# Value and filler products as two 64-column halves, one accumulator bank a unit, in a fused attention, Fourier and feed-forward layer on eight cores

## The chip, the cores and the metric

The kernel runs on the 8 cores of one Trainium2 chip, one batch element on each core, with no exchange between cores. The metric is the time of one execution on the device in microseconds (us), that of the slowest core. Engines are named as in the profile: PE is TensorE (PEld its weight loads), ACT is ScalarE, DVE is VectorE, POOL is GpSimd, SP is SyncE, which here only issues DMAs.

## The reference, cut to what matters

For each batch element, `x` is 2048 x 1024 and the context is 256 x 1024. Both are RMS-normalised and modulated by vectors computed from a condition.

```python
qx, kx, vx, fx, glx = split_in_proj(h_x @ w_in)      # 16 query heads, 4 key/value heads, width 64
kc, vc = jnp.split(h_c @ w_in[:, Q_W:V_END], 2, -1)  # context: keys and values alone
# q, k: RMS norm per head; rotary for the latent tokens
s = jnp.einsum('bqkgd,btkd->bkgqt', q_blk, k).astype(jnp.float32) * scale
p = jax.nn.softmax(s, axis=-1).astype(v.dtype)       # over 2048 + 256 keys
attn = jnp.einsum('bkgqt,btkd->bqkgd', p, v)
four = Re(fft2(fx)) per channel group                # over positions and channels
merged = g_attn * (attn @ w_attn_proj) + g_four * (four @ w_fourier_proj)
x = x + gt_m * (merged @ w_o)
x = x + gt_f * swiglu(modulate(rms_norm(x)), w_gate_up, w_down)
out = rms_norm(x, g_final)
```

## The kernel before, in words

**A planner writes the order.** The program calls helpers (`mm`, `mms`, `act`, `tt`, `load` and so on); each records a node with its engine, an assumed cost and what it reads and writes. `Tracker.schedule` then simulates the five engines and, whenever one is free, starts the ready node of lowest `prio` (its number in program order plus `late`). The order so found is written out as a fixed instruction stream for each engine; at run time each engine takes its stream strictly in order and waits at each unmet semaphore. A node of PE that carries another `mode` than the one before it is charged `SWITCH_NS` (L69). A load with `after=[v]` also waits for the last writer of `v`; without it, and with no earlier user of its buffer, it is ready at time zero. Since all helpers record one line each, a line in the profile is that of a helper: L396 is `mm` (whole 128x128 weights), L402 is `mms` (several matmuls as one node), L430 transposes, L451 ACT activations, L455 `tt` on DVE, L486 copies and L479 `stt` on DVE, L294 a DMA issue; L286 and L289 are waits.

**Opening.** Sixteen tiles of 128 tokens of `x` and two of the context are loaded on SP's queue into ten buffers `xr` (`xload`), normalised and transposed (`P1`, two tiles a call), modulated by `MOD` (four tiles a call), and projected to keys and values by `KV`. The weights (`w_ada` in four halves, then `w_kv`, `w_q`, `w_f`) come on POOL's queue. `load_tabq(0)` and `load_tabq(1)` load two tables of the queries' rotary and scale them on DVE with `stt` (L479). Four `b_ada` loads of `ada_late_rows` (256 KB each, one row broadcast to all partitions) belong to work inside the attention, but have no `after`.

**Attention.** There are 32 units (four blocks `qb` of 512 queries, eight pairs of heads `c`), each with 18 steps `kt` of 128 keys: `qk(n + 2)` makes the scores of two heads as four 64x64 matmuls (two key halves by two heads) in one of two pairs of banks; ACT takes the exponential of 128 x 1024 scores into one of seven buffers `PTs`; every second step `av(n - 1)` and `av(n)` multiply by the values and `pair_add` (DVE) adds the exponentials up in groups, for the softmax's denominators. `av` is also four 64x64 matmuls: the key rows are split in two, row half `r` accumulates in bank 4 + r. At the end of a unit `finish_unit` copies bank 4 and adds bank 5 on DVE; then come `den` (sums over partitions, as matmuls with 2 columns), `turn` and `scale`. The fillers (projections of later queries and of the Fourier branch, the DFT, the late `ada` products, part of the mixing) are called with `K.level = 2`, which gives their PE nodes the lowest priority; they use banks 6 and 7.

**Tail.** The rest of the mixing, the output projection and the feed-forward network follow, in whole 128x128 matmuls.

Of the kernel before, what the change touches and what calls it, by code (L numbers as in the profile page):

```python
# [62 lines left out]
class Tracker:  # L63
# [2 lines left out]
    LOW = 1 << 20  # L66
    MIX = 1 << 21
    LAST = 1 << 22
    SWITCH_NS = 105.0  # L69
    AHEAD_NS = 130.0  # L70

    def __init__(self):
# [227 lines left out]
def build(debug=False):  # L300
# [60 lines left out]
    def bank(b, nb=1):  # L361
        return View(PS[:, b * 512:(b + nb) * 512], "ps", b * 2048, (b + nb) * 2048)
# [4 lines left out]
    def sub(v, ap):  # L367
        return View(ap, v.sp, v.lo, v.hi)

    def rng(v, ap, elo, ehi, es_):  # L370
        return View(ap, v.sp, v.lo + elo * es_, v.lo + ehi * es_)
# [23 lines left out]
    def mm(out, lhsT, rhs, start, stop):  # L395
        return K.op("pe", lambda h: h.matmul(out.ap, lhsT=lhsT.ap, rhs=rhs.ap, start=start, stop=stop),  # L396
                    reads=[lhsT, rhs], writes=[out], cost=max(30.0, 2.0 + 0.418 * fsz(rhs)))

    def mms(parts, mode=0, cost=None):
        def fn(h):  # L400
            for o_, l_, r_, st_, sp_ in parts:
                ins = h.matmul(o_.ap, lhsT=l_.ap, rhs=r_.ap, start=st_, stop=sp_)  # L402
            return ins
        if cost is None:
            cost = sum(max(30.0, 2.0 + 0.418 * fsz(p[2])) for p in parts)
        reads, seen = [], set()
        for p in parts:
            for v in (p[1], p[2]):
                if (v.sp, v.lo, v.hi) not in seen:
                    seen.add((v.sp, v.lo, v.hi))  # L410
                    reads.append(v)
        writes, seen = [], set()
        for p in parts:
            if (p[0].lo, p[0].hi) not in seen:
                seen.add((p[0].lo, p[0].hi))
                writes.append(p[0])
        return K.op("pe", fn, reads=reads, writes=writes, cost=cost, mode=mode)

    def half(b, h):
        lo = b * 2048  # L420
        return View(PS[h * 64:(h + 1) * 64, b * 512:(b + 1) * 512], "ps", lo, lo + 2048)

    def group(b, nk, lhs, rhs, more=False):
        for k in range(nk):
            mm(bank(b), lhs(k), rhs(k), k == 0, k == nk - 1 and not more)

    def trs(pairs, ident):
        def fn(h):
# [69 lines left out]
    def load(dst, src_ap, q="sp", after=()):  # L498
        return K.dma(q, q, dst.ap, src_ap, after=after, writes=[dst], nbytes=(dst.hi - dst.lo) * 128)
# [129 lines left out]

    def load_tabq(qb):  # L630
        tq = tabqs[qb % 2]
        load(tq, ropeq_d[qb].rearrange("p (a b c) -> p a b c", a=4, b=2))
        t3 = sub(tq, tq.ap.rearrange("p a b c -> p (a b) c"))
        stt("dve", t3, t3, 0.125, sub(gq_bc, gq_bc.ap.unsqueeze(1).to_broadcast([128, 8, 64])), ALU.mult, ALU.mult)

# [17 lines left out]
    def hchunk(tb, k):  # L653
        o = tb * 4096 + k * 512
        return rng(hT, hT.ap[:, tb, k, :], o, o + 512, 2)
# [179 lines left out]
    def dft_pos(fg):  # L835
        ga = lambda a, lt: rng(G, G.ap[:, fg, a, lt, :], (fg * 4 + a) * 512, (fg * 4 + a + 1) * 512, 2)
        tab, alt, altc, GX = DF["tab"], DF["alt"], DF["altc"], DF["GX"]
        gx = rng(GX, GX.ap[:, fg, :], fg * 128, fg * 128 + 128, 2)

        yv = rng(YT, YT.ap[:, fg, :], fg * 2048, (fg + 1) * 2048, 2)  # L840
        y2 = YT.ap[:, fg, :].rearrange("p (n two) -> p n two", two=2)
        yrev = lambda lo, n: bass.AP(YT.ap.tensor, YT.ap[:, fg, lo:lo + 1].offset, [list(YT.ap.ap[0]), [-2, n]])
        for h in range(2):
            qh = dtmp[h]
            b = next_bank()
            group(b, 4, lambda k: ga(2 + h, k), lambda k: tab(2 + h, k))
            cp("act", qh, bank(b))
            b = next_bank()
            group(b, 4, lambda k: ga(h, k), lambda k: tab(h, k), more=h == 0)
            if h == 0:  # L850
                mm(bank(b), gx, alt, False, True)
            pp = bank(b)
            tt("dve", sub(yv, y2[:, 0:512, h]), pp, qh, ALU.subtract)
            if h == 0:
                tt("dve", sub(yv, yrev(2046, 511)), sub(pp, pp.ap[:, 1:512]), sub(qh, qh.ap[:, 1:512]), ALU.add)
            else:
                tt("dve", sub(yv, yrev(2047, 512)), pp, qh, ALU.add)
        px = bank(next_bank())
        mms([(sub(px, px.ap[:, 0:1]), ga(0, lt), sub(altc, altc.ap[:, 0:1]), lt == 0, False) for lt in range(4)]
            + [(sub(px, px.ap[:, 0:1]), gx, sub(alt, alt.ap[:, 0:1]), False, True)])  # L860
        cp("dve", sub(yv, YT.ap[:, fg, 1024:1025]), sub(px, px.ap[:, 0:1]))
# [72 lines left out]

    def ada_late_rows(gt, v, hf):
        g_half = rng(gt, gt.ap[:, hf * 512:(hf + 1) * 512], hf * 512, hf * 512 + 512, 4)
        load(g_half, bada_d[v * 1024 + hf * 512:v * 1024 + hf * 512 + 512].partition_broadcast(128))
        s_ = ada_next()
        pb = bank(next_bank())
        for k in range(8):  # L940
            mm(pb, sub(scond_bc, scond_bc.ap[:, k, :]), sub(s_, s_.ap[:, k, :]), k == 0, k == 7)
        tt("dve", g_half, pb, g_half, ALU.add)
        if v == 2:
            ts("dve", g_half, g_half, 0.5, ALU.mult)
# [77 lines left out]
    def av(n):  # L1022
        qb, c, kt = steps[n]
        pt = PTs[n % NPT]
        p = c // 4
        parts = []
        for r in range(2):
            for h in range(2):
                hd = 2 * p + h
                l_ = rng(V, V.ap[r * 64:(r + 1) * 64, kt, hd * 64:hd * 64 + 64], kt * 256, kt * 256 + 256, 2)  # L1030
                parts.append((half(4 + r, h), l_, sub(pt, pt.ap[r * 64:(r + 1) * 64, h * 512:(h + 1) * 512]),
                              kt == 0, kt == NKT - 1))
        mms(parts, mode=1, cost=216.0)

    sum_i = [0]
    HX = 3
# [2 lines left out]
    def pair_add(n):  # L1039
        qb, c, kt = steps[n]  # L1040
        i = kt // 2
        a, b = PTs[(n - 1) % NPT], PTs[n % NPT]
        if i == 0:
            cur["sums"] = []
        if i % HX == 0:
            slot = sums[sum_i[0] % NSUM]
            sum_i[0] += 1
            cur["sums"].append(slot)
            tt("dve", slot, a, b, ALU.add, per=0.52)
        else:  # L1050
            slot = cur["sums"][-1]
            tt("dve", slot, slot, a, ALU.add, per=0.52)
            tt("dve", slot, slot, b, ALU.add, per=0.52)

    ends = []

# [3 lines left out]

    def finish_unit(qb, c):
        xs = xss[c % 2]
        cp("dve", xs, bank(4), late=PX)
        tt("dve", xs, xs, bank(5), ALU.add, late=PX)
        ss, i = cur["sums"], c % 2
        part = [rng(rh[i], rh[i].ap[:, a, :], a * 8, a * 8 + 8, 2) for a in range(3)]

        def den():
            b = next_bank()
            K.level = 1  # L1070
            for g in range(8):
                mms([(sub(bank(b), bank(b).ap[:, g * 2:g * 2 + 2]), sub(s_, s_.ap[:, g * 128:(g + 1) * 128]),
                      sub(ones, ones.ap[:, 0, 0:2]), k == 0, k == len(ss) - 1) for k, s_ in enumerate(ss)], cost=27.0 * len(ss))
            K.level = 0
            r0, r1 = rr[i], rt[i]
            recip(r0, sub(bank(b), bank(b).ap[:, 0:16].rearrange("p (g n) -> p g n", n=2)[:, :, 0]), late=L_)
            cp("dve", part[0], r0, late=L_)
            tt("dve", r1, r0, part[0], ALU.subtract, late=L_)
            cp("dve", part[1], r1, late=L_)
            tt("dve", part[2], r1, part[1], ALU.subtract, late=L_)  # L1080

        def turn():
            b1 = next_bank()
            K.level = 1
            pt_ = sub(bank(b1), bank_bf(b1).ap[0:24, 0:128])
            trs([(pt_, sub(rh[i], rh[i].ap.rearrange("p a g -> p (a g)")))], ident)
            K.level = 0
            cp("dve", rT[i], pt_, late=L_)

        def scale():  # L1090
            b2 = next_bank()
            K.level = 1
            mms([(sub(bank(b2), bank(b2).ap[:, t * 128:(t + 1) * 128]), sub(sel, sel.ap[:, t, :]), rT[i], True, True) for t in range(4)])
            K.level = 0
            at = attnTs[qb]
            tt("dve", rng(at, at.ap[:, c, :], c * 512, c * 512 + 512, 2), xs, bank(b2), ALU.mult, late=L_)

        ends.extend(zip(DS, (den, turn, scale)))
        credit[0] -= 6
# [13 lines left out]
    PX = -300  # L1113
# [323 lines left out]
```

How the kernel before makes its waits and increments, by code:

```python
    def replay_one(self, nc, name, h, sems, dma_sems):  # L282
        for it in self.plan[name]:
            if it[0] == "wait_op":
                p = it[1]
                h.wait_ge(sems[p.eng], p.num)
            elif it[0] == "wait_dma":
                _, pool, si, val = it
                h.wait_ge(dma_sems[pool][si], val)
            else:
                n = it[1]
                if n.kind == "dma":
                    out_ap, in_ap, pool = n.dma
                    h.dma_start(out=out_ap, in_=in_ap).then_inc(dma_sems[pool][n.tk[1]], 16)
                else:
                    ins = n.fn(h)
                    if n.inc:
                        ins.then_inc(sems[n.eng], 1)
```

## Time and profile before

| | us |
|---|---|
| median of 3 runs | 1549.5 |
| lowest and highest | 1548.71, 1552.95 |
| the profiled execution | 1551.35 |
| its slowest core (core 6), first to last instruction | 1549.8 |
| its other cores | 1536.9 to 1547.7 |

The profile is that of core 6. PE is busy for 1363.4 us (88% of the span), DVE for 840.0 and ACT for 839.3 (54% each). A busy share is an average over stages that have different limits, so the stages are read one by one below: the opening, until the first exponential of the attention; the attention; and the tail. A wait is written behind an instruction as [idle time <- who ended it].

### The profile page before, as it was taken

What the parts mean: (1) busy time and instruction counts of PE and PEld (TensorE: products, weight loads), DVE (VectorE), ACT (ScalarE), POOL (GpSimd) and SP (SyncE); (2) the same over time, 40 slices, a digit from 0 to 9 for tenths busy, and PEclk for the clock granted to TensorE, in tenths of its full rate; (3) what the DMA queues carried; (4) which work ended last, traced back from release to release, by engine and by line L of the source; (5) the groups of instructions that cost most, each with busy time, mean ns of one, the idle gap of its engine ahead of it and who ended that gap; (6) DMA issues with size and microseconds to landing.
All of it is one profiled execution on the core that took longest, in us unless ns stands there. A gap on an engine that the chain in (4) does not pass through costs nothing.

```text
span 1549.8 us, 32186 instructions; the slowest of 8 cores (1536.9 to 1549.8 us)
## 1 busy us (share of the span) xinstructions
PE 1363.4 (88%) x10352; PEld 575.4 (37%) x10352; DVE 840.0 (54%) x1503; ACT 839.3 (54%) x1135; POOL 34.0 (2%) x75
## 2 busy tenths in 40 slices
PE   1267887999788798889999999998999999999997
PEld 1254232333222233223333444443444444444443
DVE  2157788898867788566776433376221112213443
ACT  4285898998877798678998222266311111111111
POOL 0000000000000000000000000000000000000000
PEclk9978899999987999979999999999999999999999
DMA  9840000011112123020122253058145232112222
GB/s 215 237 87 2 8 2 7 3 29 29 29 29 56 29 56 76 2 49 13 38 49 49 49 103 102 1 158 275 44 82 99 39 69 56 28 55 82 109 111 80
DMA packets 20795, 102.05 MB, mean 66 GB/s; under 512 B 3197, under 2 KB 3350, under 8 KB 15510
## 3 DMA queue, kind: packets, MB, share of 16 engines
q0 software_dynamic: 5616, 50.86, 17.8%
q1 hardware_dynamic: 15014, 49.14, 9.0%
q8 instruction: 86, 1.41, 0.4%
q14 instruction: 79, 0.65, 0.1%
HBM read 134.06 MB, written 16.78 MB: 97 GB/s over the span
## 4 chain that ended last, share of the span: by engine, by line
PE 70%; ACT 11%; issue 7%; DVE 6%; SPq 4%; DMA 2%; ACTq 0%; DVEq 0%; POOLq 0%; POOL 0%
PE PS L396 50%; PE PS L402 18%; ACT SB L451 10%; DVE SB L455 4%; SPq L294 4%; DMA SB<-x 2%; PE PS L430 1%; ACT SB L485 1%; DVE SB L495 0%; DVE SB L486 0%; DVE SB L471 0%; ACTq L286 0%; DVE SB L492 0%; DVEq L286 0%; DVE SB L479 0%
## 5 line engine op out<-in xcount | busy, mean ns | idle before, releaser
L396 PE MATMUL PS<-SB 128*128 128x512 bf16 x3752 | 899.5, 384 | 6.0 <-DVE SB L492 2.5
L451 ACT ACTIVATE SB<-PS 128x1024 bf16<-128x1024 f32 (+1 forms) x705 | 625.8, 963 | 319.8 <-PE PS L396 252.9
L396 PEld LDWEIGHTS PS<-SB 128*128 128x128 bf16 x3752 | 358.4, 98 | 537.6 <-issue 164.0
L402 PE MATMUL PS<-SB 64*64 64x512 bf16 (+3 forms) x6132 | 473.6, 356 | 95.4 <-ACT SB L451 51.0
L455 DVE TENSOR_TENSOR SB<-SB 128x1024 bf16<-128x1024 bf16 (+7 forms) x755 | 471.6, 645 | 88.6 <-ACT SB L451 48.2
L455 DVE TENSOR_TENSOR SB<-PS,SB 128x512 f32<-128x512 f32 (+3 forms) x262 | 173.1, 674 | 413.2 <-PE PS L396 343.6
L402 PEld LDWEIGHTS PS<-SB 64*64 64x64 bf16 (+1 forms) x6132 | 184.3, 106 | 319.1 <-issue 296.0
L451 ACT ACTIVATE SB<-SB 128x8 f32<-128x8 f32 (+4 forms) x201 | 106.2, 537 | 232.0 <-DVE SB L455 160.4
L430 PE MATMUL PS<-SB 128*128 128x128 bf16 (+1 forms) x468 | 49.3, 247 | 76.3 <-DVE SB L455 34.4
L451 ACT ACTIVATE SB<-PS,SB 128x512 f32<-128x512 f32 x64 | 44.1, 689 | 122.9 <-PE PS L396 118.4
L479 DVE SCALAR_TENSOR_TENSOR SB<-SB,PS 128x512 f32<-128x512 f32 x64 | 43.9, 686 | 101.6 <-PE PS L396 98.8
L485 ACT COPY SB<-PS 128x1024 bf16<-128x1024 bf16 (+2 forms) x91 | 66.8, 752 | 25.5 <-PE PS L430 19.2
L430 PEld LDWEIGHTS PS<-SB 128*128 128x128 bf16 (+1 forms) x468 | 34.8, 109 | 108.7 <-issue 105.8
L455 DVE TENSOR_TENSOR SB<-SB,PS 128x512 bf16<-128x512 f32 (+1 forms) x64 | 43.5, 680 | 4.5 <-PE PS L402 2.7
L479 DVE SCALAR_TENSOR_TENSOR SB<-SB 128x1024 f32<-128x1024 f32 (+2 forms) x23 | 23.5, 1028 | 37.2 <-DMA SB<-rope_q 34.3
L486 DVE COPY SB<-PS 24x128 bf16<-24x128 bf16 (+1 forms) x72 | 34.0, 472 | 3.7 <-PE PS L430 1.3
L495 DVE TENSOR_REDUCE SB<-SB 128x8 f32<-128x512 f32 x41 | 27.7, 675 | 0.0
L471 DVE TENSOR_SCALAR SB<-SB 128x512 bf16<-128x512 bf16 (+1 forms) x72 | 23.9, 399 | 3.2 <-ACT SB L485 2.3
L469 DVE TENSOR_SCALAR SB<-SB 128x1024 bf16<-128x1024 f32 (+2 forms) x19 | 12.8, 685 | 20.3 <-ACT SB L451 18.2
L492 DVE RECIPROCAL SB<-PS 128x8 f32<-128x8 f32 x32 | 6.5, 203 | 28.5 <-PE PS L402 28.3
L294 POOL DMA_DIRECT2D SB<-w_ada x12 | 6.9, 580 | 473.9 <-PE PS L402 235.2
L294 POOL DMA_DIRECT2D SB<-w_gu x11 | 5.8, 528 | 348.3 <-PE PS L396 227.3
(19 smaller groups left out, 70.9 us busy)
## 6 DMA issues: line engine op xcount, KB each, us to landing
SB<-x SPq DMA_DIRECT2D x32, 512.0 KB, 10.2
SB<-w_mix POOLq DMA_DIRECT2D x8, 1792.0 KB, 12.4
SB<-w_ada POOLq DMA_DIRECT2D x12, 1024.0 KB, 8.0
SB<-w_gu POOLq DMA_DIRECT2D x11, 1024.0 KB, 7.7
x_scratch<-SB SPq DMA_DIRECT2D x16, 512.0 KB, 4.2
SB<-x_scratch SPq DMA_DIRECT2D x16, 512.0 KB, 3.2
out<-SB SPq DMA_DIRECT2D x16, 512.0 KB, 2.6
SB<-w_dn POOLq DMA_DIRECT2D x2, 2048.0 KB, 13.6
```

The costliest lines, as they stand in the source:

```text
L294: h.dma_start(out=out_ap, in_=in_ap).then_inc(dma_sems[pool][n.tk[1]], 16)
L396: return K.op("pe", lambda h: h.matmul(out.ap, lhsT=lhsT.ap, rhs=rhs.ap, start=start, stop=stop), reads=[lhsT, rhs], writes=[out], cost=ma ...
L402: ins = h.matmul(o_.ap, lhsT=l_.ap, rhs=r_.ap, start=st_, stop=sp_)
L430: ins = h.transpose(out=o_.ap, in_=i_.ap, identity=ident.ap)
L451: return K.op("act", lambda h: h.activation(out=out.ap, in_=in_.ap, func=func, **kw), reads=reads, writes=writes, cost=ecost("act", in_), ...
L455: return K.op(eng, lambda h: h.tensor_tensor(out=out.ap, in0=a.ap, in1=b.ap, op=op), reads=[a, b], writes=[out], cost=(1600.0 if op == ALU ...
L469: return K.op(eng, lambda h: h.tensor_scalar(out=out.ap, in0=a.ap, scalar1=a1, scalar2=None, op0=op0), reads=reads, writes=[out], cost=eco ...
L471: return K.op(eng, lambda h: h.tensor_scalar(out=out.ap, in0=a.ap, scalar1=a1, scalar2=a2, op0=op0, op1=op1), reads=reads, writes=[out], c ...
L479: return K.op(eng, lambda h: h.scalar_tensor_tensor(out=out.ap, in0=a.ap, scalar=sa, in1=b.ap, op0=op0, op1=op1), reads=reads, writes=[out ...
L485: return K.op("act", lambda h: h.copy(out=out.ap, in_=in_.ap), reads=[in_], writes=w, cost=ecost("act", in_), late=late)
L486: return K.op(eng, lambda h: h.tensor_copy(out=out.ap, in_=in_.ap), reads=[in_], writes=w, cost=ecost(eng, out), late=late)
L495: return K.op("dve", lambda h: h.tensor_reduce(out=out.ap, in_=in_.ap, axis=AX.X, op=ALU.add), reads=[in_], writes=[out], cost=ecost("dve" ...
```

## The change

- `av` becomes two matmuls, one for each head, over all 128 key rows with 64 weight columns each; both accumulate in the one bank 4 + c % 2, so consecutive units take turns between banks 4 and 5. The two row halves and their two banks are gone.
- The matmuls of `group`, when called as fillers, and the last product of `dft_pos` are each issued as two matmuls of 64 weight columns over all rows (`mm_cols`) into the two partition halves of the bank. Both these and `av` carry the planner's mode 2; `qk` keeps mode 1 and whole matmuls mode 0. The planner's charge for a change of mode goes from 105 to 134 ns.
- `finish_unit` makes one copy of one bank, with the priority of the unit's other end work, and no addition.
- `pair_add` gets `late=-1500`: of the ready DVE nodes the planner takes these first.
- `load_tabq(0)` and `load_tabq(1)` wait for the last modulated chunk of tiles 4 to 7; each of the four late `b_ada` loads waits for the latest writer of `PTs[0]`.

```diff
-    SWITCH_NS = 105.0
+    SWITCH_NS = 134.0
@@
+    def mm_cols(b, l_, r_, start, stop):
+        mms([(half(b, h), sub(l_, l_.ap[:, h * 64:(h + 1) * 64]), r_, start, stop) for h in range(2)], mode=2, cost=216.0)
+
     def group(b, nk, lhs, rhs, more=False):
         for k in range(nk):
-            mm(bank(b), lhs(k), rhs(k), k == 0, k == nk - 1 and not more)
+            if K.level == 2:
+                mm_cols(b, lhs(k), rhs(k), k == 0, k == nk - 1 and not more)
+            else:
+                mm(bank(b), lhs(k), rhs(k), k == 0, k == nk - 1 and not more)
@@ def load_tabq(qb):
-        load(tq, ropeq_d[qb].rearrange("p (a b c) -> p a b c", a=4, b=2))
+        load(tq, ropeq_d[qb].rearrange("p (a b c) -> p a b c", a=4, b=2), after=[hchunk(1, 7)] if qb < 2 else [])
@@ def dft_pos(fg):
-                mm(bank(b), gx, alt, False, True)
+                mms([(half(b, z), sub(gx, gx.ap[:, z * 64:(z + 1) * 64]), alt, False, True) for z in range(2)], mode=2, cost=216.0)
@@ def ada_late_rows(gt, v, hf):
-        load(g_half, bada_d[v * 1024 + hf * 512:v * 1024 + hf * 512 + 512].partition_broadcast(128))
+        load(g_half, bada_d[v * 1024 + hf * 512:v * 1024 + hf * 512 + 512].partition_broadcast(128), after=[PTs[0]])
@@ def av(n):
-        for r in range(2):
-            for h in range(2):
-                hd = 2 * p + h
-                l_ = rng(V, V.ap[r * 64:(r + 1) * 64, kt, hd * 64:hd * 64 + 64], kt * 256, kt * 256 + 256, 2)
-                parts.append((half(4 + r, h), l_, sub(pt, pt.ap[r * 64:(r + 1) * 64, h * 512:(h + 1) * 512]),
-                              kt == 0, kt == NKT - 1))
-        mms(parts, mode=1, cost=216.0)
+        for h in range(2):
+            hd = 2 * p + h
+            l_ = rng(V, V.ap[:, kt, hd * 64:hd * 64 + 64], kt * 256, kt * 256 + 256, 2)
+            parts.append((half(4 + c % 2, h), l_, sub(pt, pt.ap[:, h * 512:(h + 1) * 512]), kt == 0, kt == NKT - 1))
+        mms(parts, mode=2, cost=216.0)
@@ def pair_add(n):
-            tt("dve", slot, a, b, ALU.add, per=0.52)
+            tt("dve", slot, a, b, ALU.add, per=0.52, late=-1500)
         else:
             slot = cur["sums"][-1]
-            tt("dve", slot, slot, a, ALU.add, per=0.52)
-            tt("dve", slot, slot, b, ALU.add, per=0.52)
+            tt("dve", slot, slot, a, ALU.add, per=0.52, late=-1500)
+            tt("dve", slot, slot, b, ALU.add, per=0.52, late=-1500)
@@ def finish_unit(qb, c):
-        cp("dve", xs, bank(4), late=PX)
-        tt("dve", xs, xs, bank(5), ALU.add, late=PX)
+        cp("dve", xs, bank(4 + c % 2), late=L_)
```

## Rows read from the trace of the kernel before

**Rows 1.** The stages: window, length, busy us (and count) of PE, PEld, DVE, ACT, POOL, PEclk, DMA share, GB/s
```profile
152.00:322.00 170.00, 147.24 (x1533) 51.80 (x1533) 142.23 (x256) 153.33 (x199) 0.35 (x1) 0.95 0.02 5
322.00:508.00 186.00, 159.97 (x1708) 55.15 (x1704) 148.01 (x286) 153.18 (x190) 2.81 (x6) 0.89 0.19 36
508.00:696.00 188.00, 159.63 (x1651) 55.05 (x1643) 138.46 (x261) 151.76 (x185) 2.11 (x4) 0.90 0.20 43
696.00:854.00 158.00, 151.65 (x1577) 50.51 (x1573) 111.44 (x212) 143.38 (x160) 1.58 (x3) 0.99 0.18 37
862.00:1549.80 687.80, 667.81 (x3199) 305.07 (x3197) 232.66 (x354) 158.86 (x261) 22.11 (x50) 0.99 0.33 87
```
**Rows 2.** The opening on SP's queue, in order of time
```profile
12.54 3.99 SPq L294 DMA_DIRECT2D SB<-rope_q  x2
16.62 29.89 SPq L294 DMA_DIRECT2D SB<-b_ada  x4
46.67 0.60 SPq L294 DMA_DIRECT2D SB<-dft_altc  x1
47.48 15.50 SPq L294 DMA_DIRECT2D SB<-x  x6
```
**Rows 3.** Landing after issue: x from 8.7 and 10.0, from 62.5; w_kv from 14.1; b_ada
```profile
L294 SPq DMA_DIRECT2D SB<-x x2: 1018/1144/1269, 8.7 to 10.0; - x2
DMA to landing us min/median/max: 41.1/44.2/47.3
...
L294 SPq DMA_DIRECT2D SB<-x x1: 502/502/502, 62.5 to 62.5; - x1
DMA to landing us min/median/max: 16.4/16.4/16.4
...
L294 POOL DMA_DIRECT2D SB<-w_kv x1: 558/558/558, 14.1 to 14.1; - x1
DMA to landing us min/median/max: 43.9/43.9/43.9
...
L294 SPq DMA_DIRECT2D SB<-b_ada x4: 6272/7666/8015, 16.6 to 38.5; - x4
DMA to landing us min/median/max: 29.8/42.6/49.7
```
**Rows 4.** The opening on DVE and PE, in order of time
```profile
27.88 0.17 DVE L455 TENSOR_TENSOR SB<-PS,SB 128x8 f32<-128x8 f32 x1
62.32 1.29 DVE L479 SCALAR_TENSOR_TENSOR SB<-SB 128x512 f32<-128x512 f32 x2 [34.27 <-DMA SB<-rope_q]
...
70.05 9.61 PE L402 MATMUL PS<-SB 128*128 128x256 bf16 x64 [2.15 <-DVE SB L471]
...
117.51 1.89 PE L396 MATMUL PS<-SB 128*128 128x512 bf16 x8 [0.62 <-ACT SB L485]
```
**Rows 5.** The first exponential, on ACT
```profile
152.11 1.03 ACT L451 ACTIVATE SB<-PS 128x1024 bf16<-128x1024 f32 x1
```
**Rows 6.** A step of the attention on PE (320 to 323 us), in order of time
```profile
321.19 0.39 PE L396 MATMUL PS<-SB 128*128 128x512 bf16 x1
321.54 0.63 PE L402 MATMUL PS<-SB 64*64 64x512 bf16 x8
322.10 0.39 PE L396 MATMUL PS<-SB 128*128 128x512 bf16 x1
322.46 0.41 PE L402 MATMUL PS<-SB 64*64 64x512 bf16 x4
```
**Rows 7.** The tail's long run of whole matmuls, in the chain that ended last
```profile
1091.40 449.81 PE PS L396 x2084
```
**Rows 8.** Groups by form: count, busy us, mean ns, idle us before them and what ended it
```profile
L451 ACT ACTIVATE SB<-PS 128x1024 bf16<-128x1024 f32 x576 | 554.0, 1044 | 58.0 <-DVE SB L486 26.3 <-PE PS L402 18.1 <-DVE SB L455 9.0
L455 DVE TENSOR_TENSOR SB<-SB 128x1024 bf16<-128x1024 bf16 x480 | 325.1, 687 | 62.7 <-ACT SB L451 40.1 <-DVE SB L455 15.1
L402 PEld LDWEIGHTS PS<-SB 64*64 64x64 bf16 x4608 | 107.7, 108 | 224.0 <-issue 209.8
L455 DVE TENSOR_TENSOR SB<-SB,PS 128x512 f32<-128x512 f32 x32 | 21.8, 681 | 1.7
```
**Rows 9.** A stall of all engines in the attention (459 to 470 us)
```profile
459.54 1.04 ACT L451 ACTIVATE SB<-PS 128x1024 bf16<-128x1024 f32 x1
...
463.40 1.29 DVE L455 TENSOR_TENSOR SB<-PS,SB 128x512 f32<-128x512 f32 x2 [2.95 <-ACT SB L451]
...
466.82 1.48 DVE L455 TENSOR_TENSOR SB<-SB 128x1024 bf16<-128x1024 bf16 x3
467.60 1.02 ACT L451 ACTIVATE SB<-PS 128x1024 bf16<-128x1024 f32 x1 [1.56 <-DVE SB L455]
```
**Rows 10.** A later table load, issued with its queue free (183 to 184 us)
```profile
L294 SPq DMA_DIRECT2D SB<-rope_q x1: 350/350/350, 183.6 to 183.6; - x1
DMA to landing us min/median/max: 2.4/2.4/2.4
```

## The prediction

> **What bounds the kernel now.** I read the busy time by stage first, because the whole-span shares hide three regimes [rows 1]. From 862 us on PE is busy for 667.8 of 687.8 us at a granted clock of 0.99. The change touches nothing there, so the tail keeps its time. In the attention (152 to 854 us, 702 us) no engine is full: adding the four stages, ACT is busy for 602 us, PE for 619 and DVE for 540, and the granted clock falls to 0.89 and 0.90 in the middle stages, that is, some stretches run at 1.2 instead of 2.4 GHz. I therefore asked next what an exponential waits for, in the groups by form [rows 8]. The third question was what fills the 152 us before the first exponential [rows 5], where the order of SP's queue shows it.
>
> *The opening.* SP issues two rope_q and four b_ada loads ahead of the last six x loads [rows 2]. The issue of b_ada alone keeps SP for 29.9 us, since the queue is full. The x load issued at 10.0 lands at 10.0 + 47.3 = 57.3 us, and the last b_ada at 38.5 + 29.8 = 68.3. So 11 us of the queue lie between two x loads. The last x load lands at 62.5 + 16.4 = 78.9 [rows 3]. A second cost is on DVE: its next instruction after 28.05 us scales the rope_q table, and waits 34.27 us for it; the normalisation of x tiles 6 and 7, the modulation and with them the first key/value matmuls (70.05 us) are behind it in the order [rows 4]. Their weights w_kv had landed at 14.1 + 43.9 = 58.0 us [rows 3].
>
> *The attention.* The 576 exponentials had 58.0 us of idle ACT before them, of which 26.3 + 9.0 = 35.3 us were ended by DVE [rows 8]. Rows 9 show the form this takes. [rows 9] After the exponential at 459.54 none starts for 8.1 us. DVE stands in its fixed order at a rotary step of a later query tile, waits 2.95 us for ACT, then works through that chain; only at 466.82 does it do the pair sums that free the exponential's output buffer, and the exponential starts at 467.60. PE, which feeds ACT, idles with it.
>
> **The change part by part.**
>
> *Loads.* Four b_ada and two rope_q loads leave the early queue. x, context and everything that follows them there move up by the 11 us that lay between 57.3 and 68.3, and DVE's 34.27 us wait is no longer ahead of the modulation. Then w_kv is the last to come, at 58.0 instead of a start at 70.05: 12 us. Both the last x (11) and the first key/value product (12) move by about the same, so the whole chain up to 152.11 should. I take -12. Bounds: -8, if the chain from 80 us on is already filled by ACT's own work; -18, because ACT also gets copies and scalings of tiles 6 to 9 done while it would wait for x (about 6 us, six such operations of some 1 us). The moved loads must be paid somewhere. The tables are needed from the first query projection, at 117.5 us now [rows 4]; one issued with its queue free landed in 2.4 us [rows 10]. On SP the waiting rope_q issue has at worst the context loads queued behind it, and on DVE its scaling stands ahead of key work: 0, at most +3. The four b_ada loads go into the attention on SP, where little is queued; DVE may wait for each at its addition, with the pair sums behind it: +1 in all, bounds 0 and 4 x 2.4 = +10.
>
> *Pair sums first.* When a sum and another DVE operation are both ready in the plan, the sum goes first. This removes stalls of the form of rows 9. It does not remove those in which DVE already waits at a PE product that comes later than planned, with the sums behind it, because the order stays fixed. I take two thirds of 35.3: -23, bounds -35 and -10. What is late next is the chain of the query rotary, which has slack, and PE.
>
> *One bank a unit.* 32 additions of 0.681 us are gone [rows 8]: 21.8 us of DVE. DVE is busy for only 540 of 702 us, so this is nothing on the path; bounds 0 and -5. The next unit's first `av` no longer waits for the copy and addition of the last, but almost none of it waits today.
>
> *Halves.* No row shows a 64-column matmul over 128 rows. The nearest are the quads of 64x64: eight of them in 322.10 - 321.54 = 0.56 us including the change to a whole matmul [rows 6]; a whole matmul takes 449.81/2084 = 0.216 us [rows 7], and two quads 0.43. So four tiles on two column halves and two row halves run together in the time of one. A pair of halves streams the same rows into the same columns, and I price it at 0.216 us as the whole matmul: 0. If the two ran one after the other, each pair would cost 0.216 more. Weight loads of 64 columns take 108 ns [rows 8] and lie beside the matmuls.
>
> The Trainium skill, "TensorEngine Tiling (Array Packing)", Gotcha 2 of its restrictions, speaks against the halves: column tiling excludes Fast Weight Load, so two half loads could replace a fast whole one. Taken one behind the other at the 108 ns of the trace they would fill 0.216 us, exactly a pair's matmul time, so the rule adds nothing that the rest would need.
>
> *Changes of mode.* A filler between quads costs 0.56 - 0.43 = 0.13 us going in and (322.46 - 322.10) - 0.216 = 0.14 coming out [rows 6], 0.135 a change. Today `qk` and `av` share a mode. I counted the changes in the PE order that the kernel's planner writes for the attention: 988. In the same order with the new modes there are 1311, for a quad of `qk` is now followed by a change even where only `av` comes, while a step with `qk`, `av` and a filler keeps its two. The 323 extra are 44 us of PE. In 69 of the 576 gaps between scores there is nothing but `av`; those have slack (0.43 + 0.27 against ACT's 0.92 a step) and hold 138 of the 323. That leaves 185 x 0.135 = 25 us; PE is the one waited for in about half of the attention, so +12; bounds 0 and +44.
>
> That moving between 64x64 tiles and 128x64 tiles is a change of mode at all is not in any row. The same page of the Trainium skill, under Key Properties, has any change of tiling mode drain TensorE; the trace agrees for 64x64 against 128x128 with its 0.13 and 0.14 us.
>
> *Clock.* In the attention the granted clock was below 1 for (0.05 x 170 + 0.11 x 186 + 0.10 x 188 + 0.01 x 158) x 2 = 99 us at half level [rows 1], at up to half of that lost. Stretches of low PE activity, as in rows 9, come before part of it. Fewer stalls: -6, bounds -20 and +10.
>
> *Sum* against the profiled execution: 1551.35 - 12 + 1 - 23 + 12 - 6 = 1523.4. The median of the runs is 1.85 below that execution, so 1521.5, told as 1521.
>
> **The rivals.**
>
> *A. The opening alone.* The switches and the fixed order eat what the sums give. For it: PE is busy for 151.7 of 158 us in the last quarter. Attention unchanged: 1549.5 - 12 = 1537.5, from 1532 to 1544.
>
> *B. Slower: PE becomes the bound through mode changes.* In a step with one filler PE now needs 0.43 + 0.216 + 0.27 = 0.916 us against ACT's 0.92 [rows 6]; any more makes PE the bound in every such step. If going to and from 128x64 costs 0.05 us more than 0.135 in 1311 places, that is 66 us, plus the 44 of the extra ones, while the removed DVE stalls lie beside it: 1549.5 - 12 + 44 + 66 - 35 = 1612. The point from which it decides is about 50 us of PE time on the path. Against it: each kind of change in the trace costs about the same. With the halves one behind the other (576 pairs of `av` and 657 of fillers at 0.216 us) it would be 266 us more, about 1790.
>
> *C. Free changes.* If the column split and not the row split makes a mode, `qk`, `av` and fillers are one: 324 changes instead of 988, 90 us less PE work, and ACT's 602 us bound the attention. It would take about 640, and the kernel 1549.5 - 12 - 62 = 1475.
>
> *D. The change does not do what it says*: the b_ada or table loads stay early by another way, or hold SP's queue for the x loads. Then the opening stays and 1533 is left.
>
> **How the numbers follow.** Forecast (1488 to 1533) 0.58; A 0.20; D 0.05; B 0.10; C 0.07. The likeliest is 1521. The range leaves out B and C and holds the rest, up to the case in which only the lower bound of the opening is left: 1488 to 1545. About 0.3% (4.6 us) can be told from no change. Faster holds the forecast, C, D and nearly all of A: 0.85. Same takes the rest of A and a mild B: 0.06. Slower 0.09.
>
> **What would show it.** The first exponential at 140 (+-4) us, with no DVE wait for rope_q of more than a few us and the last x landed before 70. In the groups, the exponentials' idle time ended by DVE at 12 us instead of 35.3. The pairs of halves starting a few ns apart, the next pair 0.216 us later. The step of one filler at 0.92 us still. A tail of 688 us. I am wrong if the pair takes more than 0.216, or if the attention is not between 665 and 695 us.

## The result, and the profile after

The changed kernel is slower: 1.0391 times the time of before, 95% interval 1.0347 to 1.0435, that is about 1610 us against 1549.5. Forecast were 1521 us and a range up to 1545. All ratios here leave out executions in which one die ran at a visibly lower clock than the other (the plain median of the changed kernel, 1661.86 us, holds two such). The profiled execution has a span of 1606.2 us on core 2.

The first fence has the stages of the changed kernel (columns as in rows 1), the second the attention as one window, for before and after: first to last exponential.

```profile
144.00:330.00 186.00, 159.24 (x1436) 57.90 (x1434) 139.49 (x252) 157.65 (x203) 0.53 (x1) 0.95 0.03 6
330.00:530.00 200.00, 167.82 (x1516) 61.49 (x1512) 138.61 (x272) 148.91 (x183) 2.64 (x5) 0.85 0.16 31
530.00:750.00 220.00, 184.32 (x1572) 66.75 (x1568) 137.16 (x258) 164.91 (x196) 2.11 (x4) 0.89 0.20 43
750.00:908.00 158.00, 151.28 (x1410) 56.20 (x1408) 103.94 (x201) 134.22 (x150) 1.58 (x3) 0.99 0.20 37
917.00:1606.20 689.20, 666.96 (x3198) 304.99 (x3194) 233.16 (x354) 158.53 (x261) 22.14 (x50) 0.99 0.34 87
```

```profile
152.10:854.90 702.80, 619.39 (x6459) 212.76 (x6459) 540.82 (x1014) 602.45 (x731) 6.85 (x13) 0.93 0.15 30
```

```profile
144.70:909.70 765.00, 663.88 (x5932) 242.97 (x5932) 520.08 (x984) 606.92 (x731) 6.87 (x13) 0.92 0.15 29
```

Of [rows 1] the tail answers as forecast: 689 us against 688. The attention grew from 702.8 to 765.0 us. ACT has the same work (602 and 607 us) and DVE 21 us less, as forecast; PE is busy for 44 us more. The longer time is idle time on ACT (100 us before, 158 now), and the granted clock is as low as 0.85 in one stage.

Two rows of the changed kernel, the exponentials' from the groups by form and the reciprocals' from the page (busy us, mean ns of one, idle us before and who ended it), then the reciprocals' of before:

```profile
L457 ACT ACTIVATE SB<-PS 128x1024 bf16<-128x1024 f32 x576 | 553.8, 1044 | 78.3 <-DVE SB L492 37.0 <-PE PS L402 21.5 <-DVE SB L461 15.5
```

```profile
L498 DVE RECIPROCAL SB<-PS 128x8 f32<-128x8 f32 x32 | 6.5, 204 | 50.5 <-PE PS L402 50.5
```

```profile
L492 DVE RECIPROCAL SB<-PS 128x8 f32<-128x8 f32 x32 | 6.5, 203 | 28.5 <-PE PS L402 28.3
```

The exponentials' idle time ended by DVE did not fall from 35.3 us [rows 8] to 12, it rose to 52.5. The reciprocal is the first DVE step after `den`. DVE's idle time before it, nearly all of it ended by PE, went from 28.5 to 50.5 us. That row leads to the cause. It was in the page of before, and the prediction did not use it.

**Opening.** SP now has the last six x loads right behind the others, and the first key/value product waits for w_kv alone. In order: the loads, PE's first key/value product and DVE, all on core 2, then the first exponential on core 6, the core of [rows 5].

```profile
13.33 34.13 SPq L294 DMA_DIRECT2D SB<-x  x6
```

```profile
59.03 9.68 PE L402 MATMUL PS<-SB 128*128 128x256 bf16 x64 [5.81 <-DMA SB<-w_kv]
```

```profile
55.37 0.74 DVE L475 TENSOR_SCALAR SB<-SB 128x1024 bf16<-128x1024 f32 x1
75.13 1.29 DVE L461 TENSOR_TENSOR SB<-PS,SB 128x512 f32<-128x512 f32 x2 [19.02 <-ACT SB L457]
```

```profile
141.48 1.03 ACT L457 ACTIVATE SB<-PS 128x1024 bf16<-128x1024 f32 x1
```

The product starts at 59.03 instead of 70.05 [rows 4], 11 us earlier as forecast. Then DVE waits 19.02 us for ACT, which takes the squares of the x tiles still arriving before that of the first keys. The last x tile landed at 70.0 us instead of 78.9. Over the eight cores the median start of the first exponential moved from 147.9 to 142.1 us: 6 us, not 12.

**A stall like that of [rows 9], in the changed kernel**, in order of time:

```profile
564.00 1.92 PE L402 MATMUL PS<-SB 128*64 128x512 bf16 x16
...
566.02 0.60 ACT L457 ACTIVATE SB<-PS 128x512 f32<-128x512 f32 x1 [3.38 <-PE PS L402]
566.72 1.29 DVE L461 TENSOR_TENSOR SB<-PS,SB 128x512 f32<-128x512 f32 x2 [1.25 <-ACT SB L457]
...
568.16 0.74 PE L402 MATMUL PS<-SB 128*128 128x2 bf16 x24 [2.24 <-DVE SB L461]
...
568.75 0.60 ACT L457 ACTIVATE SB<-SB 128x8 f32<-128x8 f32 x2 [2.13 <-DVE SB L501]
569.46 1.29 DVE L461 TENSOR_TENSOR SB<-SB 128x512 bf16<-128x512 f32 x2 [0.25 <-ACT SB L457]
...
570.67 0.20 DVE L498 RECIPROCAL SB<-PS 128x8 f32<-128x8 f32 x1
570.84 1.02 ACT L457 ACTIVATE SB<-PS 128x1024 bf16<-128x1024 f32 x1 [1.49 <-DVE SB L461]
570.85 0.69 DVE L461 TENSOR_TENSOR SB<-SB 128x1024 bf16<-128x1024 bf16 x1
```

A bank is one of the eight 512-column parts of `PS`, into which PE writes. Read backwards. The exponential at 570.84 needs its output buffer, which a pair sum must have read. That sum is the second of the two DVE operations from 569.46 on: the view merges them under the shape of the first, and they end at 570.75. The sum writes one of six slots, two units' worth, and must wait until `den` (24 matmuls with 2 columns, 568.16 to 568.90) has read that slot for the unit before last. `den` writes one of banks 6 and 7. The planner keeps the accesses to a bank in program order, so `den` waits until the filler called before it has been computed (564.00) and read out of its bank by DVE (566.72, two operations in 1.29 us). The fillers have the lowest priority and lag; as soon as they lag too far, the unit end lags with them, and two units later the exponentials stop. Call this theory W.

No exponential runs from 562.65 to 570.84. Of these 8.2 us only 1.49 are counted in front of the exponential; 3.38 and 2.13 stand in front of the two operations of a filler that ACT had ahead of it in its order. So the sum in front of the exponentials understates such stalls: of ACT's 58 us more of idle time it has 20.

In [rows 9] the two operations at 463.40 (1.29 us together) are such a read-out, not steps that happen to stand ahead of the sums. `den` follows them at once:

```profile
464.84 0.74 PE L402 MATMUL PS<-SB 128*128 128x2 bf16 x24 [2.30 <-DVE SB L455]
```

### The profile page after: what moved, and what is told of

Its sections match the earlier page's. It is cut to its first block, busy times and chain, and to the rows that moved or that the text cites. A ratio compares the mean times of both kernels' runs of the same rounds, so it can differ in the third digit from the quotient of the medians.

```text
span 1606.2 us, 31068 instructions; the slowest of 8 cores (1598.7 to 1606.2 us)
## 1 busy us (share of the span) xinstructions
PE 1408.4 (88%) x9844; PEld 606.4 (38%) x9844; DVE 818.7 (51%) x1471; ACT 843.8 (53%) x1135; POOL 34.0 (2%) x75
## 4 chain that ended last, share of the span: by engine, by line
PE 69%; ACT 12%; issue 7%; DVE 6%; DMA 4%; SPq 0%; ACTq 0%; DVEq 0%; POOLq 0%; POOL 0%
PE PS L396 39%; PE PS L402 29%; ACT SB L457 11%; DVE SB L461 4%; DMA SB<-x 4%; PE PS L436 1%; ACT SB L491 1%; DVE SB L501 1%; DVE SB L477 0%; SPq L294 0%; DVE SB L492 0%; ACTq L286 0%; DVEq L286 0%; DVE SB L485 0%; ACT L457 0%
## 5 line engine op out<-in xcount | busy, mean ns | idle before, releaser
L402 PE MATMUL PS<-SB 64*64 64x512 bf16 (+5 forms) x6268 | 690.5, 365 | 120.1 <-ACT SB L457 41.2
L396 PE MATMUL PS<-SB 128*128 128x512 bf16 x3108 | 682.8, 380 | 1.0 <-ACT SB L491 0.6
L461 DVE TENSOR_TENSOR SB<-SB 128x1024 bf16<-128x1024 bf16 (+7 forms) x755 | 464.7, 645 | 80.1 <-ACT SB L457 43.6
L402 PEld LDWEIGHTS PS<-SB 64*64 64x64 bf16 (+2 forms) x6268 | 269.9, 107 | 530.1 <-issue 489.7
L396 PEld LDWEIGHTS PS<-SB 128*128 128x128 bf16 x3108 | 302.8, 98 | 367.6 <-issue 12.1
L491 ACT COPY SB<-PS 128x512 bf16<-128x512 bf16 (+2 forms) x91 | 67.1, 752 | 28.1 <-PE PS L436 14.3
L498 DVE RECIPROCAL SB<-PS 128x8 f32<-128x8 f32 x32 | 6.5, 204 | 50.5 <-PE PS L402 50.5
L461 DVE TENSOR_TENSOR SB<-SB,PS 128x512 bf16<-128x512 f32 x32 | 21.8, 682 | 14.6 <-PE PS L402 14.6
```

Source lines behind the costliest of these rows:

```text
L461: return K.op(eng, lambda h: h.tensor_tensor(out=out.ap, in0=a.ap, in1=b.ap, op=op), reads=[a, b], writes=[out], cost=(1600.0 if op == ALU ...
L491: return K.op("act", lambda h: h.copy(out=out.ap, in_=in_.ap), reads=[in_], writes=w, cost=ecost("act", in_), late=late)
```

## The experiments

All kernels were timed against the kernel before. Two theories were put first: **M**, each change of tiling on PE costs 0.125 us on the path; **S**, the priority of the sums does the harm. Then **W**, and last **O** (the loss sits in the order that the planner writes).

**1. The edits one by one.** The loads alone, the kernel before with:

```diff
+ after=[hchunk(1, 7)] if qb < 2 else []   # load_tabq
+ after=[PTs[0]]                           # b_ada
```

> The kernel before with the two load edits alone (the rotary tables wait for the modulated chunk, b_ada for PTs[0]). Both theories: only the opening moves. In the changed kernel the first exponential came at 144.7 instead of 152.1 us, so 7.4 us earlier; here the same, 1549.5 - 7.4 = 1542 us, ratio 0.995. If the late b_ada loads hold DVE in the attention, part of it is given back and the ratio is above 0.997.

Measured 0.9951 (0.9932 to 0.9970): 7.6 us less.

```diff
+ late=-1500     # the three tt of pair_add
```

> The kernel before with late=-1500 on the pair sums alone. Theory M (changes of PE mode make the 60 us): this order has 851 changes in the attention instead of 985, at 0.125 us each 17 us less, and no stall is added: 1530 to 1545. Theory S (the sums' priority starves the rest of DVE's work, on which fillers and the unit ends wait): attention longer by 15 to 40 us, 1565 to 1590, with more idle DVE and PE.

Measured 1.0188 (1.0155 to 1.0220): 29 us more, though the order has fewer changes of tiling. M fails as the only cause. DVE's idle time before the reciprocal is 40.4 us, up from 28.5, so S names the right edit, and W offers the way: sums first means that the operations which empty banks 6 and 7 come later. (The idle time right before the exponentials is about the same, 54.9 us after 58.0. What grew is that before ACT's filler operations.)

```diff
- parts for r in 2, h in 2: half(4 + r, h), 64 rows each; mode=1
+ parts for h in 2: half(4 + c % 2, h), 128 rows; mode=2
- cp(xs, bank(4)); tt(xs, xs, bank(5))
+ cp(xs, bank(4 + c % 2), late=L_)
```

> The kernel before with the value products alone as column halves (one bank a unit, one copy); fillers stay whole, so that qk, av and fillers are three modes. The order has 1587 changes in the attention instead of 985. Theory M: 602 x 0.125 = 75 us of PE work, most of it on the path: 1600 to 1625. Theory S: the changes are hidden, as PE has idle time: 1540 to 1560.

Measured 1.0339 (1.0307 to 1.0370): 53 us more, inside M's range. The signs of W hardly moved here: 33.7 us before the reciprocal, and 36.8 us ended by DVE before the exponentials, after 35.3. PE is busy for 680 us of the attention instead of 619. So this run by itself does not show W.

```diff
+ group at K.level 2 and the last product of dft_pos by mm_cols, mode=2
```

> The kernel before with the fillers alone as column halves; av stays four 64x64 tiles. 1036 changes instead of 985: Theory M: +6 us, 1555, if a pair of halves costs the 0.216 us of a whole matmul. The changed kernel's trace has pairs that follow each other after 0.240 instead of 0.216 us: if that is the price of the halves, 655 x 0.024 = 16 us more, up to 1571. Theory S: no difference but that.

Measured 1.0054 (1.0028 to 1.0079): 8 us more, where M with halves at 0.216 us had 6. In the changed kernel filler pairs follow one another after 0.216 us (564.00 above: eight pairs in 1.92 us, of which 0.40 is the last one's own length), so the halves as such are free. The four runs add up to +82 us; the whole change, which also has the charge of 134 ns, costs 60.6. The costs do not add. One reason is plain: `av` alone makes 1587 changes of mode, while `av` and fillers together make 1338, as they share a mode. A common wait may be another.

**2. The unit end in a bank of its own.** With one bank a unit, bank 4 + c % 2 is idle once it is copied.

```diff
-            b = next_bank()      # den; likewise b1 in turn, b2 in scale
+            b = 4 + c % 2
```

> The changed kernel, with the unit-end matmuls (den, turn, scale) in the unit's own bank 4 + c % 2, which is free once it is copied, instead of the banks 6 and 7 shared with the fillers. Theory W (the exponentials stop because a pair sum waits for its slot until den has read it, and den waits in program order for a filler's bank): the exponentials' idle time ended by DVE falls from 52.5 to under 20 us, the attention from 765 to 700 to 720 us; about 145 filler products then come after the last exponential, some 31 us more there: 1570 to 1590. Theory M alone (mode changes fill PE): no change beyond 5 us.

Measured 1.0029 (1.0018 to 1.0039): 1554 us, 56 less than the changed kernel from this edit alone, more than expected. The attention took 677.5 us, and what followed the last exponential 730 instead of 696 us: by the two orders 145 filler products more come after it. First the exponentials and the reciprocals, then the attention as one window.

```profile
L457 ACT ACTIVATE SB<-PS 128x1024 bf16<-128x1024 f32 x576 | 544.1, 1052 | 9.2 <-PE PS L402 7.8
L498 DVE RECIPROCAL SB<-PS 128x8 f32<-128x8 f32 x32 | 6.4, 201 | 1.4 <-PE PS L402 1.4
```

```profile
143.80:821.30 677.50, 606.94 (x5673) 229.49 (x5673) 519.36 (x975) 589.97 (x721) 5.51 (x11) 0.96 0.13 25
```

No exponential waits for DVE any more to speak of, and of the 60.6 us some 56 are gone. That the bank shared with the fillers carries this loss is shown. The edit also makes the planner write another order, so the wait at run time and the order that plans for it are not told apart.

**3. The priority again.** The changed kernel without it:

> The changed kernel without the priority of the pair sums. Alone the priority cost 1.9% over the kernel before. If that is because it delays the DVE work that frees the fillers' banks (W), it costs here too: 15 to 25 us less, 1580 to 1590. If it only used up idle time that the mode changes now fill: within 5 us of the changed kernel.

Measured 1.0270 (1.0243 to 1.0296): 19 us less than with it. The kernel before with `late=-60` instead:

> The kernel before with the pair sums 60 places earlier instead of 1500, which puts them ahead of the DVE work of the same steps but not of that of fillers called several steps before. W: no loss, 1545 to 1556. If being first in itself does the harm (DVE stands at a sum whose exponential is late): half of the 29 us or more, 1565 and above.

Measured 0.9987 (0.9975 to 0.9998), as W had it. Being ahead of the same steps' work is harmless; it is the 1500 places, which also pass the read-outs of fillers, that cost 29 us. And with the own bank, without the priority:

> The changed kernel with the unit-end matmuls in the unit's own bank and without the priority of the pair sums. W: the priority did harm only through the wait of den for a filler's bank; with that wait gone, the priority costs nothing: within 5 us of the same kernel with the priority, 1550 to 1559. If the priority harms by itself, as over the kernel before or in the changed one: 12 to 29 us less, 1525 to 1542.

Measured 1.0034 (1.0017 to 1.0052), the same as with it (1.0029). In the changed kernel the priority harms only by way of `den`'s bank.

**4. den at the attention's priority**, in the kernel before with the loads:

```diff
-            K.level = 1          # in den
+            K.level = 0
```

> The kernel before with the two load edits and with den at the attention's own PE priority. W: den's matmuls come earlier in the order, so a slot is free sooner: 3 to 8 us less than the load edits alone (0.9951), ratio 0.990 to 0.993. M: the number of changes falls from 985 to 955, 4 us at 0.125: ratio 0.992. Both faster; it is a candidate for a version that beats both kernels.

Measured 0.9902 (0.9881 to 0.9924): a little faster than both kernels, and 8 us less than the loads alone. Its idle time before the reciprocal is 15.9 us. The ratio fits W and M alike.

**5. Whole fillers beside `av` halves**, with the own bank:

> The same as the run beside it (own bank, no priority, the planner's 134 ns) but with whole fillers, so that qk, av and fillers are three modes: 1460 changes of mode in the order instead of 1373. M: 87 x 0.125 = 11 us more. If the halves of the fillers cost something themselves (0.240 instead of 0.216 us a pair), that is saved: 508 x 0.024 = 12 us less, and the two come out equal.

Measured 1.0199 (1.0170 to 1.0227), 26 us more than its neighbour. Both expectations missed: 1460 instead of 1373 changes do not make 26 us at 0.125. Fewer filler products got into the attention (484 in the order against 508), and it was 14 us longer, the rest after it 11 us. Why stays open.

**6. What a change of tiling costs on the path.** The score product as one pair in the place of four 64x64 tiles, at an unchanged order. The kernel leaves out half of the scores, as the expectation says. In the changed kernel:

```diff
-        for kc in range(2):
-            for h in range(2):
-                ... 64x64 tile (h, kc) into bank b0 + h
+        for kc in range(2):
+            ... 128 rows, 64 columns, into bank b0 + kc
```

> The changed kernel, in exactly its order, with the score product as two matmuls of 64 columns over all 128 rows instead of four 64x64 tiles. It leaves out half of the scores (one head's lower and the other's upper half of the keys are not computed; the rest of each bank is stale) and keeps the time of the product at 0.216 us, while qk, av and the fillers are now one tiling: 350 changes instead of 1338. Theory M: the 988 removed changes at about 0.12 us are 119 us of PE, of which the attention, in steps where PE is waited for, gives back most: 60 to 100 us, 1505 to 1545. Theory W alone (the wait of den, not the changes): less than 15 us.

Two executions took 1586.1 and 1587.5 us, 20 to 25 less than the changed kernel's 1607.8 and 1610.6; there is no interval for this. Both expectations missed: M had 60 to 100 us, W less than 15.

```profile
151.60:889.50 737.90, 588.56 (x4782) 235.66 (x4782) 518.40 (x984) 600.81 (x731) 6.86 (x13) 0.94 0.15 30
```

PE is busy for 75 us less than in the changed kernel, but the attention is only 27 us shorter. The same edit with the own bank:

> The same edit on the kernel whose unit-end matmuls use the unit's own bank (1554 us): half of the scores left out, 458 changes instead of 1354, same order. The exponentials wait for no bank here. If the changes cost only through the fillers' lag and the wait of den, 896 removed ones give less than 20 us. If PE's own time sets the pace of the steps, 40 to 70 us: 1485 to 1515.

Measured 1.0009 (0.9995 to 1.0023), 3 us less than with the changes (1.0029). So M is wrong as a price: the real changes cost 20 us where the unit end shares the fillers' banks and about 3 where it doesn't. What is left for the rest of the halves' cost is the order, in which the fillers are fixed at their late places even if PE now has time. That is argued from what remains; part 7 looks at the order.

**7. The order.** The changed kernel with the planner's charge at 105:

> The changed kernel with the planner's charge for a change of mode back at 105 ns. Two runs have shown that removing 900 to 1000 real changes at an unchanged order gives only 20 and 4 us. Theory O (the order that the planner writes carries the loss: with more changes charged it puts the fillers later and the unit end behind them): a lower charge makes an order with less lag, 5 to 20 us less, 1585 to 1600. If the charge only has to be true to the chip (0.12 us), 105 is no better than 134: within 5 us of 1605, or slower.

Measured 1.0313 (1.0283 to 1.0343), 12 us less than with 134. O holds in this part: nothing on the chip was changed but the order.

The planner has a figure of its own for this, which the forecast did not read: the end time `est_ns` that `Tracker.schedule` computes together with the order. It is 1458 us for the kernel before and 1527 for the changed one, 69 more, where 61 were measured. For the priority of the sums alone it has 40 more (29 measured), for `av` alone 44 (53), for the fillers alone 8 (8). If `av` alone is given the mode of `qk`, so that no change between them is charged, it is 1457: in the plan the charged changes cost, and the products themselves nothing. The figure knows no clock and is no forecast of each kernel (the one of part 2 has +37 in it and +4.5 in the measurement), but the sign and most of the loss stand in the planned order before anything runs.

The kernel of part 4, with the charge at 134 and

```diff
-    AHEAD_NS = 130.0
+    AHEAD_NS = 0.0
```

> The fastest version so far (loads, den at the attention's priority; 0.9902) with the planner's charge at 134 ns and AHEAD_NS at 0: the planner no longer lets PE stand up to 130 ns for a score product that is about to be ready, but takes a filler. 927 changes of mode instead of 955. W and M both: less idle PE, fillers lag less, so den comes earlier: 5 to 15 us less, ratio 0.980 to 0.987. If a filler taken at that moment holds up the next scores by its 0.216 us and two changes, it is slower: above 0.992.

Measured 0.9750 (0.9726 to 0.9774), better than expected; DVE's idle time before the reciprocal is 4.7 us. The kernel of part 3 without the priority and with the own bank, AHEAD_NS 0:

> The kernel of the first run of this set with AHEAD_NS at 0: 1400 changes of mode instead of 1373. More fillers lie in the attention (552 against 508 products), so the rest after it is 44 x 0.216 = 9.5 us shorter, and the attention should not grow by as much: 1535 to 1550, against 1554 with the own bank. If the mode changes set the attention: + 27 x 0.125 + 44 x 0.216 = 13 us there, and no gain in all.

Measured 0.9801 (0.9774 to 0.9828), 1519 us, below the expectation of 1535 to 1550. And with fillers called at `RATE = 1.5` instead of 1.7 as well:

> Own bank, no priority of the sums, AHEAD_NS 0 (ratio 0.9801) with fillers called at 1.5 instead of 1.7 a step, which lowers the changes in the attention from 1400 to 1280 at the same 552 filler products in it. M: 120 x 0.12 = 14 us less, ratio 0.971, which would beat 0.975. If the number of calls does not matter: 0.980.

Measured 0.9631 (0.9603 to 0.9659), 1494 us: 56 us faster than the kernel before. The step from 0.9801 is 26 us, twice what M gave for it. Last, this kernel with the unit end back on banks 6 and 7:

> The fastest kernel (0.9631: own bank for the unit end, no priority of the sums, AHEAD_NS 0, 1.5 filler units a step) with the unit end back on the fillers' banks 6 and 7. W: the exponentials again wait for slots behind den: idle time ended by DVE back above 20 us and 40 to 55 us more, 1530 to 1550. If the other two edits made the gain, it stays within 10 us of 1494.

Measured 1.0223 (1.0197 to 1.0249), 1586 us, beyond the expectation for W. The choice of bank, the same line in three places, is worth 91 us here; the plan's `est_ns` has 54 of them (1442 and 1496). First the fast kernel, then this one, each with its exponentials and reciprocals (groups by form) and the attention as one window.

```profile
L457 ACT ACTIVATE SB<-PS 128x1024 bf16<-128x1024 f32 x576 | 557.6, 1045 | 18.5 <-PE PS L402 9.8 <-DVE SB L461 3.4 <-ACT SB L457 0.8
L498 DVE RECIPROCAL SB<-PS 128x8 f32<-128x8 f32 x32 | 6.4, 201 | 2.4 <-PE PS L402 2.4
```

```profile
146.60:771.70 625.10, 582.09 (x5761) 215.15 (x5761) 515.29 (x980) 597.32 (x724) 5.80 (x11) 0.99 0.15 30
```

```profile
L457 ACT ACTIVATE SB<-PS 128x1024 bf16<-128x1024 f32 x576 | 561.9, 1035 | 63.2 <-PE PS L402 29.4 <-DVE SB L492 18.8 <-DVE SB L461 6.6
L498 DVE RECIPROCAL SB<-PS 128x8 f32<-128x8 f32 x32 | 6.5, 204 | 28.1 <-PE PS L402 27.9
```

```profile
151.90:862.50 710.60, 632.51 (x5724) 227.23 (x5724) 518.11 (x971) 608.29 (x723) 5.80 (x11) 0.90 0.12 26
```

ACT is busy for 597 of 625 us in the fast one: the attention is now bound by it. The granted clock is 0.99 against 0.90, and PE is busy for 50 us less with the same products. The 58 fewer changes of mode are 7 us of that (an estimate at 0.12 us each); most of the rest goes with the clock.

## Why the prediction was wrong, point by point

- **Pair sums first: -23 forecast, +29 alone and +19 in the changed kernel.** This step failed in sign. The forecast took the 35.3 us ended by DVE [rows 8] for sums queued behind other DVE work. The trace names who released a wait, not what that one had waited for. In [rows 9] `den`, which reads the slot that the sum overwrites, ran from 464.84 to 465.58, and the sum began at 466.82. Of the 8.1 us a place further ahead could have saved 1.2 at most. The question left out was "what did the releaser itself wait for", and the reciprocal's 28.5 us answers it.
- **Changes of mode: +12 forecast (0 to +44), of which the halves alone cost 53 (`av`) and 8 (fillers).** The count was near: 1311 forecast, 1338 in the order. The price of one was right too: in the changed kernel a 64x64 quad to a 128x64 pair takes 0.34 us from start to start, 0.216 of it the quad. What failed is that PE's work was set against PE's idle time step by step, at an order taken as given. The order did not stay: the planner, told of 350 more changes, wrote one whose own end time is later. And the fillers may lag by two units at most before the exponentials stop, so what PE loses can come back as a stall. In the changed kernel all 988 real changes around `qk` cost 20 us (part 6), so the 350 extra ones less, and the planner's higher charge 12 (part 7). How the 53 of `av` alone divide was not measured: the signs of W hardly moved in that run, and the plan puts its 44 us down to the charged changes (part 7).
- **Opening: -12 forecast (-18 to -8), 7.6 measured alone.** The mechanism held: the key/value product came 11 us earlier. The lower bound of 8 named the case that came true, ACT's own work, and its size was a little off. Where the 7.6 us lie is less clear: with the loads alone the median start of the first exponential moved by 2 us only (147.9 to 145.9), and the rest was not located.
- **Late loads: +1 and 0, near.** The first table's scaling waits 4.43 us for rope_q, over the bound of 3; how much of it reached the first exponential was not measured. No DVE wait for b_ada shows.
- **Halves at full rate: right.** Pairs follow at 0.216 us. The rule of the Trainium skill on Fast Weight Load ("TensorEngine Tiling (Array Packing)", Gotcha 2) can't be told from these rows, since the loads lie beside the matmuls; the rule that a change of tiling mode drains the engine (same page, Key Properties) agrees with the 0.12 us for 64x64 against 128x64, which no row of before had shown.
- **One bank a unit: 0 forecast, right as the change uses it.** Its worth is that it frees a bank for the unit end, which the change does not use.
- **Clock: -6 forecast.** At half level in the attention: 99 us before, 130 in the changed kernel, 55 with the own bank, 14 in the fastest. The time at half level rose instead of falling. In these four the clock goes with the stalls, but not in all: sums first alone had 96 us at half level and was 29 us slower. What the clock adds by itself was not separated.
- **Rival B** had the sign and the place (extra changes). That its 1612 us is near the 1610 measured is luck: it needs 0.05 us more for each change, which is not there, and 110 us of PE time on the path, where the real changes cost 20.

## What to carry to other kernels

When an engine ends a wait, follow that engine's own wait one step further back, down to the buffer or bank, before pricing a change of priority. Work of low priority must not share a bank, slot or queue with work that the critical loop will need later, as the shared order turns its lag into a stall. A program whose order is fixed by a planner has to be judged by the order it gets: a small change of an assumed cost moved 12 us, and removing about 1000 real changes at an unchanged order 20 or 3. Such a planner's own end time, before and after, is the first number to compare.

## What the runs showed of the hardware that was not expected

Between a 64x64 quad and a 128x64 pair a change costs as much as to whole weights (0.10 to 0.14 us either way): keeping the column split alike on both sides saves nothing. The next rows are of the changed kernel, whole, quad and pair, whole, quad.

```profile
559.67 0.39 PE L396 MATMUL PS<-SB 128*128 128x512 bf16 x1
559.99 0.75 PE L402 MATMUL PS<-SB 64*64 64x512 bf16 x6
560.67 0.39 PE L396 MATMUL PS<-SB 128*128 128x512 bf16 x1
560.99 1.16 PE L402 MATMUL PS<-SB 64*64 64x512 bf16 x10
```

From 559.67 to 560.99 there are four products (0.216 us each) and four changes in 1.32 us, 0.11 us a change. Against [rows 6], the step of one filler went from 0.92 to 1.00 us where the filler is still a whole matmul.
